# First block's projections: from f32 products to three float32r passes over split operands, on one Trainium2 core

## What is computed

```python
h = rmsnorm(x, norm_mix_g)
proj = h @ w_in                                   # [256, 1024] x [1024, 7424]
qkv_a, q_b, k_b, v_b, gate_logits = jnp.split(proj, split_at, axis=-1)
# three groups of dilated window attention (8 heads of 64), merged by their log sums
og, lg = dilated_window_attention(qg, kg, qkv_a[:, :, 2, gi], window, dil)
o_a = jnp.sum(wts[..., None] * jnp.stack(outs, axis=0), axis=0)
o_b = gqa_blocked_attention(qb, kb, vb)           # 8 query heads, 2 key/value heads
gates = jax.nn.sigmoid(gate_logits.reshape(b, s, N_BRANCHES, d) + b_gate)
merged = gates[:, :, 0] * (o_a @ w_proj_a) + gates[:, :, 1] * (o_b @ w_proj_b)
x = x + merged @ w_out
h2 = rmsnorm(x, norm_ffn_g)
ff = moe_ffn(h2, w_router, b_router, ...)         # top 4 of 32 experts
x = x + ff
```

## Time and profile before

| | |
|---|---|
| median of 3 runs | 2218.21 us (2218.15 to 2218.84) |
| the profiled execution | 2219.3 us, its span 2217.5 us, mean granted clock 0.966 |
| TensorE busy | 2054.3 us, 93% of the span |
| VectorE, ScalarE, GpSimd busy | 969.9, 300.8, 87.9 us |
| chain that ended last, by engine | PE 86%, DVE 7%, issue 3%, POOL 1%, ACT 1% |
| L711, the f32 products of the first block | 544 matmuls in a group, busy 244.9 us, 12% of the chain |

### The profile page before, as it was taken

One profiled execution on the slowest core, in us unless ns is written; L12 is line 12 of the kernel. 1 busy time (PEld: TensorE's weight loads), 2 busy tenths in 40 slices (PEclk: granted clock), 3 DMA queues, 4 the chain that ended last, 5 costly groups with the idle time before them and its releaser, 6 DMA issues.

```text
span 2217.5 us, 24206 instructions
## 1 busy us (share of the span) xinstructions
PE 2054.3 (93%) x9832; PEld 1259.3 (57%) x9832; DVE 969.9 (44%) x1570; ACT 300.8 (14%) x526; POOL 87.9 (4%) x107
## 2 busy tenths in 40 slices
PE   7989999999999999999999999997879997988996
PEld 4444664544444444444444447866858885766885
DVE  3321333422332333332233234646667676657765
ACT  1111440111010111101101012211100000211000
POOL 2210000000000000000000000104200000000000
PEclk9988999899999999999999999998989998989998
DMA  9423123599999999999999994430225454424551
GB/s 367 144 76 114 46 82 131 228 424 426 428 427 428 428 428 427 428 428 427 428 428 427 428 428 157 142 124 1 77 76 190 152 192 150 152 76 171 171 193 54
DMA packets 106013, 560.13 MB, mean 253 GB/s; under 512 B 5856, under 2 KB 11232, under 8 KB 81248
## 3 DMA queue, kind: packets, MB, share of 16 engines
q1 hardware_dynamic: 102528, 551.61, 62.1%
q10 hardware_dynamic: 3424, 7.67, 1.0%
HBM read 558.21 MB, written 1.05 MB: 252 GB/s over the span
## 4 chain that ended last, share of the span: by engine, by line
PE 86%; DVE 7%; issue 3%; POOL 1%; ACT 1%; DMA 0%; ACTq 0%; SPq 0%; POOLq 0%; DVEq 0%
PE ps L952 20%; PE ps L711 12%; PE ps L979 10%; PE ps L992 7%; PE ps L993 7%; PE ps L994 7%; PE ps L928 6%; PE ps L917 3%; PE ps L1041 2%; PE ps L1049 1%; PE ps L747 1%; PE ps L1121 1%; PE ps L780 1%; PE ps L1135 1%; PE ps L969 1%
## 5 line engine op out<-in xcount | busy, mean ns | idle before, releaser
L952 PE MATMUL ps<-ring,arena 128*64 128x512 f32 x2048 | 447.5, 595 | 0.0
L952 PEld LDWEIGHTS ps<-ring,arena 128*64 128x64 f32 x2048 | 144.4, 137 | 286.9 <-issue 286.9
L979 PE MATMUL ps<-ring,arena 128*64 128x512 f32 x1024 | 226.8, 594 | 26.6 <-ACT arena L1424 26.6
L711 PE MATMUL ps<-ring,actT 128*128 128x512 f32 (+1 forms) x544 | 244.9, 604 | 1.8 <-DMA ring<-in_w_in_dram 1.7
L1991 DVE TENSOR_SCALAR arena<-ps 128x512 f32<-128x512 f32 x32 | 22.1, 691 | 504.5 <-PE ps L952 504.5
L992 PE MATMUL ps<-split_w,act_parts 128*128 128x512 f32 (+1 forms) x544 | 218.4, 401 | 25.2 <-DVE act_parts L1608 25.2
L993 PE MATMUL ps<-split_w,act_parts 128*128 128x512 f32 (+1 forms) x544 | 213.4, 392 | 0.0
L994 PE MATMUL ps<-split_w,act_parts 128*128 128x512 f32 (+1 forms) x544 | 212.7, 391 | 0.0
L1608 DVE TENSOR_TENSOR split_w<-ring,split_w 128x2048 fp32r<-128x2048 f32 (+2 forms) x92 | 198.1, 2153 | 3.2
L711 PEld LDWEIGHTS ps<-ring,actT 128*128 128x128 f32 x544 | 104.1, 197 | 124.0 <-issue 120.8
L979 PEld LDWEIGHTS ps<-ring,arena 128*64 128x64 f32 x1024 | 84.6, 137 | 146.6 <-issue 114.9
(11 more groups left out here) (299 smaller groups left out, 2168.9 us busy)
## 6 DMA issues: line engine op xcount, KB each, us to landing
ring<-in_w_gate_up_dram SPq DMA_DIRECT2D x128, 2048.0 KB, 16.6
ring<-in_w_down_dram SPq DMA_DIRECT2D x64, 2048.0 KB, 13.3
ring<-in_f_w_dram SPq DMA_DIRECT2D x28, 2048.0 KB, 7.9
ring<-in_w_in_dram SPq DMA_DIRECT2D x14, 2048.0 KB, 11.0
ring<-in_a_w_in_dram SPq DMA_DIRECT2D x8, 2048.0 KB, 8.0
ring<-in_b_w_qkv_dram SPq DMA_DIRECT2D x6, 2048.0 KB, 7.9
ring<-in_f_w_dram SPq DMA_DIRECT2D x4, 1536.0 KB, 6.9
ring<-in_w_out_dram SPq DMA_DIRECT2D x2, 2048.0 KB, 7.8
```

The source lines that it names most:

```text
L711: mm = pe.matmul(ps[:, bank, 0:n], lhs(k), slot_ap[:, k, :], start=(k == 0), stop=(k == kn - 1))
L952: mm = pe.matmul(ps[half, bank, :], xeT[:, 2 * c + j, :], w[:, j, at:at + 512], start=False, stop=(c == 3 and j == 1), skip_group_check=True)
L979: mm = pe.matmul(ps[half, 3, :], act_eT[:, j, (c - 4) * BLK:(c - 3) * BLK], w[:, j, n * 512:(n + 1) * 512], start=(c == 4 and j == 0), sto ...
```

## The change

The products of chunks 2 to 14, the projections and the output products become three float32r passes over high and low parts. Chunks 0 and 1 stay f32. Of each load from 2 on, ScalarE writes the rounded copy (`cast_half`) and VectorE the rest (`low_half`), in two halves of 128x2048, at the places that `splits_at` gives: both halves of loads 3 to 9 behind tile 0 of the chunk before, both halves of loads 10 to 16 behind tile 1 of the chunk two before, loads 17 and 18 in the output stage. The parts of even loads lie in `split_w[0]` and of odd ones in `split_w[1]`, which take the room of ring slots 2 to 5; the raw loads alternate between slots 1 and 0 (load 2 in slot 4), and SyncE issues load L + 2 when load L is split. The turned activations get a high part from ScalarE and a low one from VectorE. The projections run all of b first, then all of a. The gates' bias comes in four DMAs of 512, issued by ScalarE, instead of one. The split of the experts' bias moves on VectorE from before the residual to behind `hot_rows(1)`. Some semaphores are merged.

```diff
+LOAD_K = [KD] * PROJ_LOAD + [4, 4, KD, KD]
+LOAD_N = [w[3] for w in W_CHUNKS] + [D, D, 512, 512]
+FULL_K = [8, 8, 0] + [0] * 5 + [0] * (PRE_LOADS - 8)
+def raw_slot(load):
+    return (1, 0, 4)[load] if load < 3 else (1, 0)[(load - 3) % 2]
+def splits_at(c, tile):
+    if c == 0:
+        return [(2, tile)]
+    return [s for s in SPLITS if s[0] > 2 and s[0] <= PROJ_LOAD + 1 and
+            ((s[0] - 1, 0) if s[0] < 10 else (s[0] - 2, 1)) == (c, tile)]
...
@@ sync @@
             def load(i, src):
+                if i >= 3:
+                    last = i - 3 if i < 5 else i - 2
+                    if FULL_K[last]:
+                        sync.wait_ge(gemm_ready, 2 * last + 2)
+                    if FULL_K[last] < LOAD_K[last]:
+                        sync.wait_ge(pre_split, splits_done(last, 1))
...
             for c in range(RING):
+                if c < 2:
+                    sync.wait_ge(pre_split, splits_done(OUT_LOAD + c, 1))
+                else:
+                    sync.wait_ge(gemm_ready, G_OUT + 2 + c // 2)
...
@@ tensor @@
+            def products(g, load, lhs, parts, k0, k1, at, n):
...
                 for k in range(k0, k1):
+                    if k < FULL_K[load]:
+                        mm = pe.matmul(dst, lhs(k), slot(slot_, kn, LOAD_N[load])[:, k, at:at + n], **edge)
+                    else:
+                        if k in (0, kn // 2):
+                            pe.wait_ge(pre_split, splits_done(load, int(k > 0)))
+                        mm = exact(dst, parts(k), [part_place(load, i, kn, LOAD_N[load])[:, k, at:at + n]
+                                    for i in range(2)], **edge)
...
-            pe.wait_ge(oT_ready, 4)
+            for b in range(2):
+                for tile in range(NT):
+                    pe.wait_ge(oT_ready, 2 * b + tile + 1)
+                    s_ = slice(tile * P, (tile + 1) * P)
+                    for n in range(2):
+                        products(G_PROJ + 4 * b + 2 * tile + n, PROJ_LOAD + b, None,
+                                 lambda k: (oT_parts[:, 0, b, k, s_], oT_parts[:, 1, b, k, s_]),
+                                 0, 4, n * 512, 512)
...
@@ scalar @@
+            def cast_half(load, half):
...
+                    elif load == OUT_LOAD:
+                        act.wait_ge(gemm_ready, G_PROJ + 4)
+                    elif load == OUT_LOAD + 1:
+                        act.wait_ge(gemm_ready, G_PROJ + 8)
+                    elif load > 3:
+                        act.wait_ge(gemm_ready, 2 * (load - 2) + 2)
+                act.activation(part_place(load, 0, kn, n)[:, s_, :],
+                               slot(raw_slot(load), kn, n)[:, s_, :], ACT.Copy).then_inc(pre_cast, 1)
...
                         act.activation(s, s, ACT.Sigmoid).then_inc(gates_ready, 1)
+                        if tile and group < 3:
+                            act.dma_start(gate_rows, everyone("b_gate", 512 * group + 512, 512))
+                    for load, half_ in splits_at(c, tile):
+                        cast_half(load, half_)
...
@@ vector @@
+            def low_half(load, half):
...
+                dve.wait_ge(pre_cast, splits_done(load, half))
+                dve.tensor_tensor(part_place(load, 1, kn, n)[:, s_, :],
+                                  slot(raw_slot(load), kn, n)[:, s_, :],
+                                  part_place(load, 0, kn, n)[:, s_, :], ALU.subtract)\
+                    .then_inc(pre_split, 1)
...
+            for tile in range(NT):
+                for b in range(2):
+                    dve.tensor_tensor(pre_low[s_], xT[s_], pre_high[s_], ALU.subtract)
...
+                    for load, half_ in splits_at(c, tile):
+                        low_half(load, half_)
...
+            for i in range(4):
+                tile, n = divmod(i, 2)
+                g = G_PROJ + i
+                dve.wait_ge(gemm_ready, g + 1)
+                dve.tensor_tensor(merged[:, tile, n * 512:(n + 1) * 512], ps[:, g % GB, :],
+                                  gates[:, tile, D + n * 512:D + (n + 1) * 512], ALU.mult)\
+                    .then_inc(gemm_free[g % GB], 1)
+            for half in range(2):
+                low_half(OUT_LOAD, half)
+            for i in range(4):
...
+                dve.wait_ge(gemm_ready, g + 1)
+                dve.tensor_tensor(part, ps[:, g % GB, :], gates[:, tile, n * 512:(n + 1) * 512],
+                                  ALU.mult).then_inc(gemm_free[g % GB], 1)
+                read_out(dve, g)
+                dve.tensor_tensor(dst, dst, part, ALU.add).then_inc(merged_ready, 1)
...
+            for half in range(2):
+                low_half(OUT_LOAD + 1, half)
```

More of the change, by code:

```diff
@@ L378, in program @@
         part = area(2048, 512)
[L379 removed]
+        xT = area(6144, KD, S)
+        gate_rows = area(17408, 512)
         sumsq, rstd = small[:, 0:16], small[:, 16:32]
@@ L1589, in after, with turn_out @@
                 dve.wait_ge(v_step, n)
-            def turn_out(first, tile, gain):
+            def turn_out(first, tile, gain, into=actT):
                 for b in range(2):
@@ L1670, in _ @@
             after(tables)
+            for tile in range(NT):
+                for b in range(2):
+                    s_ = (slice(None), slice(4 * b, 4 * b + 4), slice(tile * P, (tile + 1) * P))
+                    dve.wait_ge(act_high_done, 2 * tile + b + 1)
+                    dve.tensor_tensor(pre_low[s_], xT[s_], pre_high[s_], ALU.subtract)\
+                        .then_inc(x_split, 1)
             inverted = {}
@@ new lines, in _ @@
+            dve.wait_ge(gates_ready, 8)
+            for i in range(4):
[5 more added lines that the diff above has]
+                    .then_inc(gemm_free[g % GB], 1)
+            for half in range(2):
+                low_half(OUT_LOAD, half)
@@ new lines, in _ @@
+            for tile in range(NT):
+                for b in range(2):
+                    s_ = (slice(None), slice(4 * b, 4 * b + 4), slice(tile * P, (tile + 1) * P))
+                    dve.wait_ge(act_high_done, 8 + 2 * tile + b + 1)
+                    dve.tensor_tensor(pre_low[s_], ps[:, 4 + 2 * tile + b, :]
+                                      .rearrange("p (k n) -> p k n", n=P), pre_high[s_],
+                                      ALU.subtract).then_inc(turn_done, 1)
+            for half in range(2):
+                low_half(OUT_LOAD + 1, half)
@@ L1978, in _ @@
             hot_rows(1)
+            dve.wait_ge(raw_bias_in, 64)
+            c = step.on(dve.tensor_copy(bias_parts[:, :, :], raw_bias))
+            after(c)
+            for q in (1, 3):
+                low_rows = slice(NE * q, NE * q + NE)
+                ins = dve.tensor_tensor(bias_parts[low_rows], raw_bias[low_rows],
+                                        bias_parts[low_rows], ALU.subtract)
+            ins.then_inc(bias_split, 1)
             dve.wait_ge(m_gathered, 1)
```

193 lines of the change are left out of this document (98 added, 95 removed).

## The result

| | before | after |
|---|---|---|
| median of four runs | 2218.18 us (2217.2 to 2218.84) | 2266.49 us (2265.02 to 2267.78) |
| profiled execution / its span | 2219.3 / 2217.5 us | 2265.0 / 2263.2 us |
| mean granted clock | 0.966 | 0.944 |
| TensorE busy | 2054.3 us (93%) | 2034.0 us (90%) |
| VectorE / ScalarE busy | 969.9 / 300.8 us | 1048.6 / 367.8 us |

The ratio is 1.0215, with a 95% interval of 1.0203 to 1.0228: slower, by 48.3 us. The forecast was 2261 us, its range 2230 to 2290.

What follows compares the result with a forecast made beforehand. The prediction took TensorE to bound the rewritten first 393 us, but expected it to wait for splits queued ahead of VectorE's reading out. Terms 22.3 + 22.5 + 8.0 - 9.6 gave +43.2 us: 2261 us, range 2230 to 2290.

Steps and rivals of the forecast that it cites:

- Prices: All split products: 48.6 us of TensorE time saved; each load costs two copies of 1.91 us and two subtracts, 4.64 us.
- Start to the first such wait: Start through chunk 5: VectorE sets the pace, scores at 113.1 us where they were at 104.85, +8.2 us.
- Chunks 6 and 7: These two head chunks: a period of 24.4 us against 23.7, +1.4 us for both.
- the value stage: Value chunks 8 to 10: new waits for reading out behind the splits, 12.7 us up to the first gate half.
- Gate chunks 11 to 14: Gate steps: scores wait behind the split, then low clock; +22.5 us for chunks 11 to 13, +8.0 for chunk 14.
- Projections to the residual: Output stage: 52.3 us where it took 61.9, -9.6 us.
- Costed at nothing: Raw loads, the router's moved bias split and the first expert's later loads: no added time; experts unchanged.
- Sum: Whole kernel: 22.3 + 22.5 + 8.0 - 9.6 = +43.2 us, so the median becomes 2261.4 us.
- (a): Rival for the whole change: splitting hides and TensorE keeps its saving, 2169.6 us; chance 0.09.
- (b): Rival at the new waits: they cost only themselves, no further low clock, 2233 us; chance 0.2.
- (c): Rival at the waits: low clock lasts, 4.8 us instead of 2.8 each, 2286 to 2292 us; chance 0.17.
- (d): Rival at the products: the three passes do not come at 0.227 us, nothing is saved, 2301 us; chance 0.03.

Runs made afterwards that it cites:

- e1: Changed kernel with the splits of chunks 10 and 11 issued behind tile 0 of chunks 9 and 10, half a chunk sooner: 2252.11 us.
- e4: Changed kernel with eight unused float32 products added on TensorE ahead of the scores at the second, third and fourth gate step: 2257.08 us.
- e6: Changed kernel with only ScalarE's split copy cut to 8 columns of each row from chunk 4 on (results invalid): 2250.87 us.
- e2: e1's edit, plus the gate chunks' splits (loads 12 to 15) spread by halves over the attention steps of the chunk before: 2198.76 us.
- e10: e8 with load 5's split back behind tile 0 of chunk 4 and load 11's behind attention step 7: 2191.89 us, 0.9873 of the kernel before.
- e5: Changed kernel with split copy and subtract both cut to 8 columns of each row from chunk 4 on (results invalid): 2195.43 us.
- e7: Changed kernel with only VectorE's split subtract cut to 8 columns of each row from chunk 4 on (results invalid): 2228.87 us.
- e8: e2 with loads 5 to 11 split a whole chunk ahead, behind the attention step that ends the chunk two before: 2196.00 us.
- e3: e2 with the subtract of the next chunk's second half moved behind the attention step that ends chunks 3 to 7: 2198.68 us.

## Why the prediction was right, point by point

- **Prices.** The copy was "not in the trace", taken at 1.91 us between 1.06 and 2.5; it measures 1.904 (34 of them, 1.892 to 1.921). The estimate by the Trainium skill (ScalarE: Activation LUTs, What ACT_TABLE_LOAD costs), 1.89, agrees too. The subtract, from 2.292, is 2.291. The passes came 0.23 apart; a warm gate step is 6.41 for 7.07, 0.65 less where I had 0.72.
- **Start to the first such wait.** Predicted +8.2, measured +6.2. TensorE's wait for the second head tile ends at 35.25 us (L864, 4.02 us), forecast 36.3. The difference lies in the execution and not in the forecast: in e1, e4 and e6, which are the same program up to there, that wait ends at 36.66 to 36.78 us and scores(2) come at 112.85 to 112.98, +8.0 to +8.1. Part of it is the arrival of the first weights: over the eleven traces the first products start between 12.12 us (here) and 13.27.
- **Chunks 6 and 7.** Predicted period 24.4, measured 24.1 (135.26 to 159.29, 24.0); 23.7 before. With the value stage it makes +21.4 at the first gate half, where +22.3 was forecast: scores(5) at 181.41 (184.5 forecast), scores(6) at 202.35 (206.5). The stage itself cost a little more than I gave it: +14.5 from scores(4) to the gate half, against 12.7. The mechanism held, and e1 shows it by removal for two of the three waits.
- **Gate chunks 11 to 14.** Scores "at 10.35", measured 274.96 - 265.42 = 9.54. More than half of the difference, 0.46 of 0.81, is the bias DMA, which I had added: its 0.34 us of issue lies beside the table load (266.52, inside 266.46 to 267.74) and costs nothing. The rest is that each split instruction starts a little before the one ahead has ended. The low clock behind the wait was taken at 2.8 us; it is 2.5, 3.4 and 3.8. The misses nearly cancel, which is luck: 2.4 us too much for the three waits, 1.3 too little for the clock behind them, and 1.0 too little for 15 half products that save 0.65 us each and not 0.72. The stage is 136.5 us for 106.1, +30.3, and +30.5 was forecast (22.5 + 8.0). The transposes come at 382.54, forecast 383.6.
- **Projections to the residual.** -9.6 forecast, 51.9 us for 61.9 measured.
- **Costed at nothing.** Held: TensorE waits 1.0 us for the ring's DMA, loads land in 7.8 us (median), the experts' period is 29.14 us in both, and the first expert product lags by 41.85 us, as the residual does (41.8), so the moved bias split costs nothing there.
- **Sum.** +43.2 forecast, +41.8 at the residual, +45.7 in the spans. The step that was missed is "from there the program is unchanged": it is, but its time is not, 3.9 us more. The last section finds nearly all of it where the clock is lower in the same rows. The forecast is 5 us under the median of 2266.5: 2.5 us of that in the spans, the rest in that the profiled executions are not the median ones.
- **Rivals.** (a), that the splitting hides, did not hold, and by the same token the rule of the Trainium skill (Perfetto Trace Analysis, Identifying the Most-Contended Engine) did not lead to the time: the most occupied engine got less work (2034 us busy in all) and the kernel became slower. The reason I gave against it, "the place in the queues", is borne out: with other places, e2 and e10 come 19 and 26 us under the kernel before. Its 2170 us were not reached by any run: even with nearly free splits in the old places (e5) only 23 of the 48.6 us are kept. (b) is refuted by e4. (c) was partly right: the low clock costs more at the later steps, 3.8 us at the third, but nowhere 4.8. (d) is refuted by the step of 6.41 us.
- **Luck.** The mechanism was right at each stage; that the total came within 5 us owes something to misses of either sign that offset each other, in the gate chunks and ahead of them (up to scores(4) 2.7 us too much, in the value chunks 1.8 too little).

What stays open: why the clock stays low for 5.4 us behind one wait of 7.43 us and for 8.3 behind another, and whether the 6.8 us in e10 can be spread over more chunks.

## What to carry to other kernels

When work is taken off the busiest engine and given to idle ones, find the short instruction on each of those which the busy engine waits for, and see what now stands ahead of it in the queue; the idle share does not tell. Place the new work behind that instruction; in the gate chunks it went in halves, the consumer one step behind the producer (no run tells whether the halves or the distance matter by themselves): the same 34 copies and 34 subtracts cost 48 us in one order and brought 26 in another. Price a wait of TensorE with the clock behind it, which at the gate steps came to 2.5 to 3.8 us behind waits of 4.9 to 7.4 us, and still to 1.6 to 3.2 behind waits of 1.5 to 1.6.

## What I had not expected of the hardware

**Idle time costs more than itself, and filling it with useless products pays** (e4): 7.03 us of added products in each of three waits made the kernel 9.4 us faster.

**The clock can fall in code that has not changed.** The last 3.9 us of the difference are 1.0 us in the first expert block (its first 64 matmuls take 15.95 us for 14.96, the granted clock over 30 us from there is 0.93 for 0.97) and some 2.9 us behind the last expert. The same rows of both kernels, the kernel before first:

```profile
1354.75 3.64 PE L1025 MATMUL ps<-small,actT 128*128 128x16 f32 x32
1358.24 10.61 PE L1041 MATMUL ps<-actT,ring 128*128 128x256 f32 x48
```

```profile
1397.57 4.64 PE L1079 MATMUL ps<-small,actT 128*128 128x16 f32 x32
1402.05 12.96 PE L1095 MATMUL ps<-actT,ring 128*128 128x256 f32 x48
```

The gaps ahead of them are the same in both (0.78 and 1.38 us), the granted clock over these 48 matmuls is 1.00 before and 0.82 after. Over all eleven kernels this group took 10.61 us in five (the kernel before, e2, e7, e8, e10), 12.29 in two (e3, e5) and 12.88 to 13.01 in four (the changed kernel, e1, e4, e6), and no run here was made to separate the cause. From the first expert product to the end, in which no run changes anything, the eleven traces take 1800.1 to 1806.1 us (1802.0 in the kernel before, 1805.9 in the changed one, 1806.1 in e4, 1800.1 to 1801.2 in e2, e3, e5, e7, e8 and e10). So up to 6 us of a difference between two whole times may come from there, and a difference of a few us is better read at a landmark just behind the edit. By the first expert product e3 is 0.4 us ahead of e2, and e8 2.4.
